# Act tiles of eight of eleven up-projection steps computed as seven products of halves

## What is computed

```
def conv_ffn(h, w_up, w_dw, b_dw, w_down):        # w_up (1024, 2 * 2816), w_down (2816, 1024)
    up = jnp.einsum("bsd,df->bsf", h, w_up)
    act, gate = up[..., :D_FF], up[..., D_FF:]
    act = causal_dwconv(act, w_dw, b_dw)          # width 3, along the tokens
    return jnp.einsum("bsf,fd->bsd", jax.nn.silu(act) * gate, w_down)

x = x + conv_ffn(rmsnorm(x, norm_ffn[i]), ffn_w_up[i], ffn_w_dw[i], ffn_b_dw[i], ffn_w_down[i])
```

## Time and profile before

| | |
|---|---|
| Median of 3 executions | 939.38 us (938.29, 939.38, 939.70) |
| Span of the profiled execution (first to last instruction) | 937.5 us |
| Own time of the profiled execution | not given apart from its span; the median is 1.9 us above the span |
| PE busy | 926.4 us, 99% of the span |
| DVE, ACT, POOL busy | 542.8, 365.8, 87.0 us |
| Chain that ended last | PE 95%, DVE 2%, POOL 1%, issue 1% |
| HBM read | 86.1 MB |

### The profile page before, as it was taken

One profiled execution on the slowest core, in us unless ns is written; L12 is line 12 of the kernel. 1 busy time (PEld: TensorE's weight loads), 2 busy tenths in 40 slices (PEclk: granted clock), 3 DMA queues, 4 the chain that ended last, 5 costly groups with the idle time before them and its releaser, 6 DMA issues.

```text
span 937.5 us, 12821 instructions
## 1 busy us (share of the span) xinstructions
PE 926.4 (99%) x5028; PEld 778.3 (83%) x5028; DVE 542.8 (58%) x689; ACT 365.8 (39%) x479; POOL 87.0 (9%) x78
## 2 busy tenths in 40 slices
PE   8999999999999999999999999999999999999997
PEld 7888888888888888888888898888888888888887
DVE  6999986576555556654343468755555555532333
ACT  7653566443333333332222454533333333322331
POOL 0575824000000000000000020000000000000000
PEclk9999999999999999999999999999999999999999
DMA  7323030222233222221323331322222232223212
GB/s 256 118 90 113 12 106 28 108 90 91 89 100 118 95 89 89 95 88 62 121 68 118 110 135 51 130 89 89 89 89 89 95 116 74 80 83 114 92 62 90
DMA packets 18558, 89.66 MB, mean 96 GB/s; under 512 B 2528, under 2 KB 5856, under 8 KB 11488
## 3 DMA queue, kind: packets, MB, share of 16 engines
q1 hardware_dynamic: 17952, 88.72, 27.8%
q10 hardware_dynamic: 576, 0.52, 0.2%
HBM read 86.09 MB, written 2.10 MB: 94 GB/s over the span
## 4 chain that ended last, share of the span: by engine, by line
PE 95%; DVE 2%; POOL 1%; issue 1%; SPq 0%; DMA 0%; ACT 0%; DVEq 0%; POOLq 0%
PE bank L1127 28%; PE bank L1128 28%; PE bank L1129 28%; PE bank L1169 1%; PE bank L1204 1%; PE bank L1187 1%; DVE sumsq L1091 1%; DVE h_lo L1057 1%; SPq L306 0%; PE bank L1193 0%; PE bank L1221 0%; PE bank L1461 0%; PE bank L1493 0%; PE bank L1465 0%; PE bank L1466 0%
## 5 line engine op out<-in xcount | busy, mean ns | idle before, releaser
L1127 PE MATMUL bank<-h_hi,w_hi 128*128 128x512 f32 x784 | 306.1, 390 | 0.0
L1129 PE MATMUL bank<-h_hi,w_lo 128*128 128x512 f32 x784 | 305.0, 389 | 0.0
L1128 PE MATMUL bank<-h_lo,w_hi 128*128 128x512 f32 x784 | 305.0, 389 | 0.0
L493 ACT ACTIVATE w_hi<-w_raw 128x2048 fp32r<-128x2048 f32 (+2 forms) x87 | 147.3, 1693 | 232.0 <-PE bank L1129 231.1
L796 DVE TENSOR_TENSOR w_lo<-w_raw,w_hi 128x2048 fp32r<-128x2048 f32 (+2 forms) x81 | 162.1, 2002 | 100.8 <-ACT w_hi L493 100.0
L1127 PEld LDWEIGHTS bank<-h_hi,w_hi 128*128 128x128 f32 x784 | 147.2, 188 | 31.3 <-issue 0.5
L1129 PEld LDWEIGHTS bank<-h_hi,w_lo 128*128 128x128 f32 x784 | 147.1, 188 | 30.8
L1128 PEld LDWEIGHTS bank<-h_lo,w_hi 128*128 128x128 f32 x784 | 147.2, 188 | 30.6 <-issue 0.5
L1128 PE MATMUL bank<-u_lo,w_hi 128*128 128x512 f32 (+1 forms) x406 | 153.3, 378 | 0.0
L1127 PE MATMUL bank<-u_hi,w_hi 128*128 128x512 f32 (+1 forms) x374 | 141.0, 377 | 0.0
L1129 PE MATMUL bank<-u_hi,w_lo 128*128 128x512 f32 (+1 forms) x374 | 140.8, 377 | 0.0
(11 more groups left out here) (208 smaller groups left out, 914.8 us busy)
## 6 DMA issues: line engine op xcount, KB each, us to landing
w_raw<-w_up SPq DMA_DIRECT2D x44, 1024.0 KB, 4.8
w_raw<-w_down SPq DMA_DIRECT2D x32, 704.0 KB, 4.0
w_raw<-w_pw SPq DMA_DIRECT2D x11, 1024.0 KB, 5.2
x_res<-x SPq DMA_DIRECT2D x3, 512.0 KB, 7.3
out<-out_sb SPq DMA_DIRECT2D x12, 128.0 KB, 1.8
w_raw<-w_pw SPq DMA_DIRECT2D x4, 256.0 KB, 6.9
gathered<-stage SPq DMA_DIRECT2D x32, 32.0 KB, 2.3
w_raw<-w_pool SPq DMA_DIRECT2D x2, 512.0 KB, 3.7
```

Source lines behind the costliest of these rows:

```text
L493: nc.scalar.activation(w_hi[s][:, 0:columns], w_raw[s][:, 0:columns], ACT.Copy).then_inc(w_rounded[s], 1)
L1127: M.matmul(dst, a, hi, start=start, stop=False)
L1128: M.matmul(dst, a, lo, start=False, stop=False)
L1129: return M.matmul(dst, b, hi, start=False, stop=stop)
```

## The change

In each layer the first three up steps (`PLAIN`) stay as they were. In the other eight (`FAST`) the act pair is computed in Strassen's form (Winograd's variant): the 1024x256 weight block and the 512 tokens are each cut in two along every dimension, and seven products of halves (4 chunks by 3 passes, 12 matmuls of 256 columns each) give what eight halves of the plain form give. PE does 84 matmuls of 256 columns and 48 of 512 in such a step. Each product stands between two of the eight chunks of the gate pair (`TURNS`). The products go into bank 4 (products 1, 6, 7, 4) and bank 5 (5, 3, 2), and are combined while they accumulate and by ACT and DVE (`copy_first`, `copy_fifth`, `copy_second`, `copy_low`; the two ADDs in DVE's `fast_step`).

The input has to be the normed activation itself, in halves and differences of halves: DVE makes it in plain step 0 (`scale_h`, eight operations of 128x512) and plain step 1 (`add_mixed`, `split_mixed`, four of 128x1024 each); ACT rounds (`round_mixed`, `round_as_is`) and POOL makes the rests of the unmixed halves (`split_as_is`). The scaling of `y` and of the act tiles by the factor falls away in the fast steps. The seven weight operands of a fast step (128x512 each) are sums that DVE makes from the raw weights (`add_weights`, four of them), rounded by ACT (`round_op`) and split by DVE (`split_op`), in a ring of four slots that lies in the place of `w_hi[0]` and `w_lo[0]`. The gate pair's weights keep slot 1 and are rounded and split in two halves (`round_gate`, `split_gate`). `u_hi` of the last 16 chunks is written only at the end of the up steps, by ACT (`round_late`), and `u_lo` by POOL (`split_late`), since their place holds the mixed input before. Buffers of other stages move to other addresses. The loops over the up steps are unrolled on each engine.

The diff, cut to its core (`...` where lines are left out; the order: constants, buffers, SP, ACT, DVE, PE):

```diff
+PLAIN = 3
+FAST = UP_STEPS - PLAIN
+UNIT_HALF = UNIT // 2
...
+ORDER = (1, 5, 6, 3, 7, 2, 4)
+PRODUCTS = len(ORDER)
+PLACE = {product: n for n, product in enumerate(ORDER)}
+RING = 4
+TURNS = ((None, 0), (1, None), (None, 1), (5, None), (None, 2), (6, None), (None, 3), (3, None), (None, 4), (7, None),
+         (None, 5), (2, None), (None, 6), (4, None), (None, 7))
+MIXED = {5: 0, 6: 1, 7: 2, 4: 3}
...
+        ring_hi = [place(f"ring_hi{n}", [P, KH, P], f32r, RING_AT + 4096 * n) for n in range(RING)]
+        ring_lo = [place(f"ring_lo{n}", [P, KH, P], f32r, RING_AT + 4096 * n + 2048) for n in range(RING)]
+        ring_sum = [place(f"ring_sum{n}", [P, KH, P], f32, RING_AT + 4096 * n + 2048) for n in range(RING)]
...
-        v_hi, v_lo = u_lo[:, 0:KD, :], u_lo[:, KD:2 * KD, :]
+        v_hi, v_lo = h_hi, h_lo
...
+        def slot_free(queue, layer, i, n):
+            done = job(layer, i, n) - RING + 1
+            if done > FAST * layer * PRODUCTS:
+                queue.wait_ge(product_done, done)
+            else:
+                queue.wait_ge(unit_done[0], M_UP[layer] + PLAIN)
...
+                for i in range(PLAIN, UP_STEPS):
+                    before, source = step_of(layer, i), 2 * (i + UP_STEPS * layer)
+                    for u in range(2):
+                        if i == PLAIN:
+                            sp.wait_ge(w_split[u], M_UP[layer] + PLAIN)
+                        elif u == 0:
+                            sp.wait_ge(sum3, before)
+                            sp.wait_ge(op_split, job(layer, i - 1, PLACE[1]) + 1)
+                        else:
+                            sp.wait_ge(gate_split, 2 * before - 1)
+                        sp.dma_start(w_raw[u][:, 0:UNIT_HALF], w_up[source + u][:, 0:UNIT_HALF]).then_inc(near_loaded[u], 16)
+                    for u in range(2):
+                        if i > PLAIN and u == 0:
+                            sp.wait_ge(op_split, job(layer, i - 1, PLACE[4]) + 1)
+                        elif i > PLAIN:
+                            sp.wait_ge(gate_split, 2 * before)
+                        sp.dma_start(w_raw[u][:, UNIT_HALF:UNIT], w_up[source + u][:, UNIT_HALF:UNIT]).then_inc(far_loaded[u], 16)
+                sp.wait_ge(sum3, FAST * (layer + 1))
...
+            def plain_step(layer, i):
...
+                if i == PLAIN - 1:
+                    for n in range(4):
+                        round_op(layer, PLAIN, n)
+                    round_gate(layer, PLAIN, 0)
+                    round_gate(layer, PLAIN, 1)
...
+            def round_gate(layer, i, half):
+                step, at_half = step_of(layer, i), slice(half * UNIT_HALF, (half + 1) * UNIT_HALF)
+                act.wait_ge((far_loaded if half else near_loaded)[1], 16 * (step + 1))
+                if i == PLAIN:
+                    act.wait_ge(unit_done[1], M_UP[layer] + PLAIN)
+                else:
+                    act.wait_ge(gate_done, 2 * step - 1 + half)
+                nc.scalar.activation(w_hi[1][:, at_half], w_raw[1][:, at_half], ACT.Copy).then_inc(gate_rounded, 1)
...
+            def fast_step(layer, i):
+                last, after = i == UP_STEPS - 1, step_of(layer, i) + 1
+                if i > PLAIN:
+                    silu(layer, i - 1, 1)
+                    round_gate(layer, i, 1)
+                copy_first(layer, i)
+                copy_fifth(layer, i)
+                round_op(layer, i, PLACE[7])
+                round_op(layer, i, PLACE[2])
+                copy_second(layer, i)
+                round_op(layer, i, PLACE[4])
+                if last:
+                    for c in range(8):
+                        round_late(layer, c)
+                else:
+                    round_op(layer, i + 1, PLACE[1])
+                    round_op(layer, i + 1, PLACE[5])
+                    round_gate(layer, i + 1, 0)
+                    round_op(layer, i + 1, PLACE[6])
+                act.wait_ge(edge_added, after)
+                conv_middle(layer, i, 0)
+                if last:
+                    for c in range(8, 12):
+                        round_late(layer, c)
+                copy_low(layer, i)
+                if last:
+                    act.wait_ge(product_done, FAST * (layer + 1) * PRODUCTS)
+                    round_unit(0, M_DOWN[layer], DOWN_UNIT)
+                act.wait_ge(corner_added, after)
+                act.wait_ge(low_copied, after)
+                conv_middle(layer, i, 1)
+                silu(layer, i, 0)
+                if not last:
+                    round_op(layer, i + 1, PLACE[3])
+                else:
+                    for c in range(12, 14):
+                        round_late(layer, c)
+                    silu(layer, i, 1)
+                    act.wait_ge(gate_done, 2 * after)
...
+            def plain_step(layer, i):
...
+                if i == 0:
+                    scale_h(layer)
+                if i == 1:
+                    for product in (5, 6, 7, 4):
+                        add_mixed(layer, product)
+                if i == PLAIN - 1:
+                    build_ahead(layer)
...
+                if i == 1:
+                    for product in (5, 6):
+                        split_mixed(layer, product)
+                if i == PLAIN - 1:
+                    for half in range(2):
+                        split_gate(layer, PLAIN, half)
...
+            def scale_h(layer):
+                norm = "ffn0" if layer == 0 else "ffn1"
+                for c in range(KD):
+                    V.scalar_tensor_tensor(as_is_whole[c // KH][:, :, 1, c % KH, :], x_res[:, c, :].rearrange("p (h t) -> p h t", h=2), col(norm, c), rms[:, :].rearrange("p (h t) -> p h t", h=2), MUL, MUL).then_inc(h_scaled, 1)
...
+            def build_ahead(layer):
+                split_op(layer, PLAIN, 1)
+                add_weights(layer, PLAIN, 5)
+                add_weights(layer, PLAIN, 6)
+                split_op(layer, PLAIN, 5)
+                add_weights(layer, PLAIN, 3)
+                split_op(layer, PLAIN, 6)
+                split_op(layer, PLAIN, 3)
...
+            def fast_step(layer, i):
+                last, after = i == UP_STEPS - 1, step_of(layer, i) + 1
+                if i > PLAIN:
+                    use_gate(layer, i - 1, 0)
+                    split_gate(layer, i, 1)
+                    use_gate(layer, i - 1, 1)
+                add_weights(layer, i, 7)
+                split_op(layer, i, 7)
+                split_op(layer, i, 2)
+                split_op(layer, i, 4)
+                dve.wait_ge(product_done, job(layer, i, PLACE[7]) + 1)
+                dve.wait_ge(fifth_copied, after)
+                if not last:
+                    split_op(layer, i + 1, 1)
+                V.tensor_tensor(act_in[:, 1, 2 + HT:2 + T], bank[BANK_LOW][:, 0:HT], fifth, ADD).then_inc(corner_added, 1)
+                if not last:
+                    add_weights(layer, i + 1, 5)
+                dve.wait_ge(product_done, job(layer, i, PLACE[2]) + 1)
+                dve.wait_ge(second_copied, after)
+                V.tensor_tensor(act_in[:, 0, 2:2 + T], bank[BANK_EDGE][:, :], first_two, ADD).then_inc(edge_added, 1)
+                if not last:
+                    add_weights(layer, i + 1, 6)
+                    split_op(layer, i + 1, 5)
+                    split_gate(layer, i + 1, 0)
+                conv_rest(layer, i, 0)
+                if last:
+                    split_unit(0, M_DOWN[layer], DOWN_UNIT)
+                else:
+                    add_weights(layer, i + 1, 3)
+                    split_op(layer, i + 1, 6)
+                conv_rest(layer, i, 1)
+                if not last:
+                    split_op(layer, i + 1, 3)
+                else:
+                    use_gate(layer, i, 0)
+                    use_gate(layer, i, 1)
+                    split_unit(1, M_DOWN[layer], DOWN_UNIT)
...
+            def product(layer, i, which):
...
+                half = slice(HT, T) if which in (5, 3) else slice(0, HT)
+                dst = bank[BANK_LOW if which in (1, 6, 7, 4) else BANK_EDGE][:, half]
...
+                for k in range(KH):
+                    a, b = ring_hi[slot][:, k, :], ring_lo[slot][:, k, :]
+                    M.matmul(dst, a, hi[:, k, :], start=which in (1, 5) and k == 0, stop=False, skip_group_check=True)
+                    M.matmul(dst, a, lo[:, k, :], start=False, stop=False, skip_group_check=True)
+                    last = M.matmul(dst, b, hi[:, k, :], start=False, stop=which in (2, 3, 4) and k == KH - 1, skip_group_check=True)
+                last.then_inc(product_done, 1)
...
+            def gate_chunk(layer, i, k):
...
+                if k % KH == 0:
+                    pe.wait_ge(gate_split, 2 * step + k // KH + 1)
...
+                for i in range(PLAIN, UP_STEPS):
+                    for which, k in TURNS:
+                        if which is None:
+                            gate_chunk(layer, i, k)
+                        else:
```

(1 more changed line is left out.)

344 lines of the change are left out of this document (272 added, 72 removed).

## The result

The changed kernel takes 966.14 us (median of 4, 964.45 to 967.27) against 939.54 us of the kernel before: ratio 1.0288, 95% interval [1.0272, 1.0303], **26.6 us slower**. The forecast was 949, with a range to 960: the sign was right, the size was not, and the time lies above the range.

The account below looks back on a forecast made before the run. PE was taken as the bound, busy 99% of the 937.5 us span. Saving 12.8 and pauses of 6.8, 8.8 and 6.8 gave +9.6, so 947.1, plus 1.9: 949 us, range 942 to 960.

Parts of the forecast that it names:

- Plain step 1: Second up step of each layer: added DVE and ACT work delays slot 1's next split to 21.8, needed after 21.76; pause 0.
- POOL's two rests: POOL's rests of the unmixed halves, 4.6 us each, start at 14.6 and end by 26, long before use: free.
- Rival 1: PE's clock falls to half rate in the pauses, adding 7.5 (956.5 us) to 15 (964 us); chance 0.15.
- (a): Plain step 0: `scale_h` delays the split of slot 1's weights; PE pauses 2.4 and 4.4 us, together 6.8.
- (b): Entry to the fast steps: gate half 0 waits for slot 1's release, then for busy DVE; pause 4.4 us, twice 8.8.
- my lower end of 2.5: Lower bound of each entry pause: only rounding and splitting gate half 0 after slot 1's release, at least 2.5 us.
- DVE's own layout: DVE's predicted work up to the entry: two multiplications done at 35.9, gate half 0 split at 37.05, PE ready at 32.7.
- (c): Exit from the fast steps: first down unit rounded only after product 4, behind ACT's late chunks; pause 3.4 us, twice 6.8.
- The saving: PE's gain in the fast steps: each lasts 20.96 instead of 21.76 us, so 16 save 12.8 us.
- Rival 2: Fast steps are paced by DVE, gate half 0 late by 0.2 to 0.7 a step: +3 to +10 us; chance 0.13.
- the margin of 0.7: In a fast step, DVE finishes splitting the next step's gate half 0 at 20.25, due at 20.96: margin 0.7 us.
- my 9.6: Net forecast change over the whole kernel: -12.8 + 6.8 + 8.8 + 6.8 = +9.6 us.

Follow-up runs that it names:

- experiment 2: The changed kernel, but POOL writes zeros as the rests of the unmixed halves, reading nothing (part of the result left out): 955.06 us, ratio 1.0182.
- experiment 9: The kernel with DVE's work in order of need (934.29 us), but the second unmixed half's rest made on POOL again: 935.95 us, ratio 0.9968.
- experiment 1: The changed kernel with matmuls that nobody reads, on an idle bank, filling PE's eight pauses: 960.69 us, ratio 1.0242.
- experiment 3: The changed kernel with `scale_h` moved behind the split of slot 1's weights in plain step 0: 966.31 us, ratio 1.0305.
- experiment 4: The changed kernel, but each layer's fast steps begin with products 1 and 5 and end with gate chunks, first down unit rounded earlier: 953.21 us, ratio 1.0154.
- 5: The changed kernel with experiment 4's turns, preparation reordered, unmixed rests on DVE, and a changed exit (DVE splits six late chunks): 941.78 us, ratio 1.0034.
- 6: As 5, but with the exit of experiment 4, all late chunks on POOL without a hold: 941.78 us, ratio 1.0035.
- 4 to 9: Includes two runs not named singly: 5 with DVE's work ordered by PE's need, 934.29 us; that with some operand and gate splits earlier, 932.92 us.

## Why the prediction was right or wrong

- **"Plain step 1 ... So 0, with nothing to spare", with "POOL's two rests ... free".** This is the step that failed, by 7.4 us of pauses and some 2.5 of half rate (9.9 together, experiment 2). I asked when POOL's result is needed, not what POOL's reading does to DVE meanwhile. No row of before could show it: in that trace no DVE operation with two SBUF inputs begins while one of POOL's subtractions runs, and rows 11 gave me POOL's own 4.6 alone. The Trainium skill has the rule ("SBUF — State Buffer", "SBUF: two separate sides"): a DVE operation with two SBUF inputs and a GpSimd operation that reads SBUF exclude each other, and whichever starts first holds the shared ports for its whole instruction. Experiments 2 and 9 agree with it at 8.27 against 1.29 us and 3.53 against 0.75, and so do the operations with a PSUM input, which aren't hit. Read against the diff, it would have pointed at this place. With no half rate in it (experiment 1) the term is 5.27 + 5.24 = 10.5 us, where my sum has 0.
- **Rival 1, the clock, chance 0.15.** It came true, behind seven pauses, and is worth 4.3 us (experiment 1), 7.5 to 15 in my text. I had multiplied a slow stretch by the number of pauses; four of the seven are covered by the next wait for DVE. It wasn't independent of the forecast: with pauses of 2.4 and more, as the runs now show, it belonged in the sum.
- **(a), 6.8.** Right: 6.95, at the place and with the releaser named, 2.45 and 4.50 for 2.4 and 4.4. Experiment 3 shows the limit of such a term: the same work moved behind the split costs as much one step later, so "2.4 us of pause" was the price of that place, not of the work.
- **(b), 8.8.** 5.4. Each is 2.71 and not 4.4, only the rounding and the split of gate half 0, near my lower end of 2.5. DVE's own layout held: in experiment 2 it had the multiplications done 35.4 us after PE's release in step 0 (35.9 in the forecast), and in experiment 1, with no half rate, the pause is 4.15 and 4.13. In the changed kernel the slow stretch behind step 2's pause (1.64 and 1.69) brings PE later to that point, and by then DVE is ready. The clock and this term lie on one path: some 3 of the 11.6 us of half rate stand in place of what is missing here.
- **(c), 6.8.** 5.7; the mechanism held (experiment 4), and three of DVE's taps about each exit took 1.65 to 1.78 beside POOL's late splits, which I hadn't seen, while the split itself kept its 1.62.
- **The saving, 12.8.** 10.6. The products have their 0.120 (297.44 - 296.01 = 1.43 for twelve), but a gate chunk takes 298.83 - 297.44 = 1.39 for six, 0.2317 each and not 0.2267; eight of them make the step 0.2 longer. The changed gate chunk reads the tokens as two pieces of 256. That alone doesn't explain it: the third of each three passes reads them so too and is followed after 0.226 to 0.228, the first two after 0.232. No run settles it.
- **Rival 2**, fast steps paced by DVE: wrong, no pause stands inside a fast step of the changed kernel, in spite of the margin of 0.7.

In the terms of the forecast: -10.6 + 6.95 + 7.36 + 5.42 + 5.73 = 14.9, 5.3 above my 9.6; half rate is the other 11.6 of the 17 us missed. Of it experiment 1 gives back only 4.3, since PE's slow stretches and DVE's lateness share a path. Its own sum, 20.9, is the fairer test of the rest: 11.3 above my 9.6, of which step 2 is 10.5 and the saving 2.2, less 1.6 by which (b) and (c) were too high.

## What to carry to other kernels

POOL's work was free here only where it neither read SBUF beside a DVE operation with two SBUF inputs that PE waited for, nor was late itself; check each added GpSimd instruction against both. On a kernel where PE is the bound, added preparation costs what it puts in front of the split PE waits for next, so order it by need date. A single move pays in full where no later wait inherits the delay (experiment 4, 11.8 us) and nothing where one does (experiment 3, and the exit between 5 and 6). Here the same arithmetic went from 2.9% slower to 0.7% faster by its order and by which engine does it.

## What the runs showed of the hardware

- Over the changed kernel and experiments 2, 3, 4 and 9, 25 pauses of PE were 2.45 to 9.92 us, and behind 21 of them matmuls stood 0.427 apart (512 columns) or 0.213 (256), for some 3 to 3.7 us (5.7 in experiment 9), an excess of 1.4 to 1.75 (2.8); in 1 and 4 to 9, 41 pauses (or remainders behind dummies) of 0.28 to 1.97 us in the same stages had none (one of 0.40 in the first up step, which every kernel has, isn't counted). The four exceptions were all 2.71 to 2.87 us long, a length that elsewhere did have it. The excess doesn't grow with the pause (1.53 behind 7.93, 1.63 behind 2.45). My forecast said that nothing showed what a pause of this length does among dense work; now rows do. The Trainium skill ("TensorE: Matmul & The Clock Gate", "Why this matters for your kernels") says that idle gaps between bursts of matmuls throw the clock back; these rows agree.
- One long POOL instruction shuts DVE out once and wholly (3.53 for 0.75). Sixteen short ones slow each of DVE's operations (1.67 for 0.75, 2.71 for 1.62) in the same way: DVE waits for one of them, then POOL for DVE, turn by turn. POOL's 128x2048 subtraction has such waits in its record too: its 5.04 in the changed kernel and 5.65 in experiment 9 are 4.45 and 4.46 counted from the end of the DVE operation that ran when it began, against 4.6 undisturbed.
